# Twelve split weight slots of a two-block transformer kernel, moved from one byte residue modulo 512 to twelve

## The reference

```python
def _swiglu(t, w_gate, w_up, w_down):
    return (jax.nn.silu(t @ w_gate) * (t @ w_up)) @ w_down

def first_block(x, mem, ...):
    for l in range(DEPTH):                                  # DEPTH = 2
        h = h + 0.5 * _rmsnorm(_swiglu(...ffn1...), ...)    # 1024 -> 2816 -> 1024
        proj = u @ w_in[l]                                  # three kinds of attention
        ...
        merged = g_sb * (o_sb @ w_br_sb) + g_fx * (o_fx @ w_br_fox) + g_mem * (o_mem @ w_br_mem)
        h = h + _rmsnorm(merged @ w_out[l], ...)
        h = h + 0.5 * _rmsnorm(_swiglu(...ffn2...), ...)

def second_block(x, ...):
    # layer 0: short convolution mixer; layer 1: latent attention; each with a
    # convolutional FFN: (silu(g) * u) @ w_down, where g, u = conv(x_n @ w_up)
    ...
    return rms_norm(h, final_norm)
```

## Time and profile before

| | |
|---|---|
| median of 3 runs | 1845.45 us (1845.1 to 1845.69) |
| span of the profiled execution | 1842.3 us |
| TensorE matmul | 1829.0 us busy, 99%, 10951 instructions |
| TensorE weight load | 1633.5 us busy, 89% |
| VectorE | 1287.1 us, 70% |
| ScalarE | 1090.7 us, 59% |
| GpSimd | 205.1 us, 11% |
| DMA | 333.94 MB, mean 181 GB/s |

### The profile page before, as it was taken

How to read it: one execution, slowest core, us unless ns; L and a number is a source line. 1 busy time by engine, 2 the same in 40 slices (tenths; PEclk the granted TensorE clock), 3 DMA queues, 4 the chain that set the end, 5 groups by cost and what they waited for, 6 DMA issues and landing times.

```text
span 1842.3 us, 28823 instructions
## 1 busy us (share of the span) xinstructions
PE 1829.0 (99%) x10951; PEld 1633.5 (89%) x10951; DVE 1287.1 (70%) x2041; ACT 1090.7 (59%) x1885; POOL 205.1 (11%) x158
## 2 busy tenths in 40 slices
PE   8999999999999999999999999999999999999998
PEld 7888999998888888888999888888889998989997
DVE  6775747787777568755777788755768765768763
ACT  7665545555666466645555657655557654757653
POOL 0220001110022002200011102210002210001210
PEclk9999999999999999999999999999999999999999
DMA  9755565455576558664654548654747654537663
GB/s 268 216 186 183 172 194 171 140 158 176 173 225 192 189 148 233 186 193 139 196 176 143 186 146 230 193 190 144 226 139 215 187 195 155 173 115 205 198 192 103
DMA packets 435721, 333.94 MB, mean 181 GB/s; under 512 B 25338, under 2 KB 381312, under 8 KB 435584
## 3 DMA queue, kind: packets, MB, share of 16 engines
q1 hardware_dynamic: 435008, 331.57, 59.7%
q10 hardware_dynamic: 576, 0.53, 0.1%
HBM read 330.97 MB, written 1.05 MB: 180 GB/s over the span
## 4 chain that ended last, share of the span: by engine, by line
PE 96%; DVE 2%; ACT 1%; issue 0%; DMA 0%; ACTq 0%
PE bank L1759 16%; PE bank L1736 15%; PE bank L1738 15%; PE bank L1737 15%; PE bank L1747 7%; PE bank L1761 7%; PE bank L1748 7%; PE bank L1749 7%; PE bank L1765 2%; PE bank L1758 1%; DVE wlo L1106 1%; PE bank L2017 0%; DVE U L1159 0%; PE bank L2083 0%; PE bank L2088 0%; PE bank L2054 0%
## 5 line engine op out<-in xcount | busy, mean ns | idle before, releaser
L1106 DVE TENSOR_TENSOR wlo<-raw,whi 128x1024 fp32r<-128x1024 f32 (+3 forms) x637 | 760.9, 1202 | 286.3 <-ACT whi L578 276.8
L578 ACT ACTIVATE whi<-raw 128x1024 fp32r<-128x1024 f32 (+3 forms) x637 | 645.6, 1023 | 324.6 <-PE bank L1738 247.9
L1759 PE MATMUL bank<-U,whi 128*128 128x512 f32 x1280 | 439.2, 395 | 0.2 <-DVE wlo L1106 0.2
L1761 PE MATMUL bank<-U,wlo 128*128 128x256 f32 x1120 | 314.6, 281 | 0.0
L1747 PE MATMUL bank<-U,whi 128*128 128x256 f32 x1024 | 289.2, 282 | 0.0
L1748 PE MATMUL bank<-U,whi 128*128 128x256 f32 x1024 | 286.1, 279 | 0.0
L1749 PE MATMUL bank<-U,wlo 128*128 128x256 f32 x1024 | 286.0, 279 | 0.0
L1759 PEld LDWEIGHTS bank<-U,whi 128*128 128x128 f32 x1280 | 230.2, 188 | 42.9 <-DVE wlo L1106 0.7
L1736 PE MATMUL bank<-whi,U 128*128 128x384 f32 (+2 forms) x592 | 219.2, 370 | 2.7 <-DVE wlo L1464 2.1
L1736 PE MATMUL bank<-whi,hhi 128*128 128x512 f32 x560 | 219.3, 392 | 0.0
L1738 PE MATMUL bank<-wlo,hhi 128*128 128x512 f32 x560 | 218.1, 390 | 0.0
(11 more groups left out here) (309 smaller groups left out, 2367.4 us busy)
## 6 DMA issues: line engine op xcount, KB each, us to landing
raw<-in_ffn_w_up SPq DMA_DIRECT2D x351, 256.0 KB, 3.5
raw<-in_ffn_w_down SPq DMA_DIRECT2D x264, 256.0 KB, 2.9
raw<-in_ffn_w_gate SPq DMA_DIRECT2D x175, 256.0 KB, 3.4
raw<-in_w_gate SPq DMA_DIRECT2D x128, 192.0 KB, 2.9
raw<-in_w_in SPq DMA_DIRECT2D x80, 256.0 KB, 3.4
raw<-in_a_w_in SPq DMA_DIRECT2D x48, 256.0 KB, 3.2
raw<-in_w_mem_kv SPq DMA_DIRECT2D x32, 256.0 KB, 3.3
raw<-in_w_out SPq DMA_DIRECT2D x32, 256.0 KB, 3.1
```

The lines of the kernel that those rows point to most:

```text
L578: act.activation(whi[n % SLOTS][:, 0:w], raw[n % RAW][:, 0:w], ACT.Copy).then_inc(hi_ready, 1)
L1106: dve.tensor_tensor(wlo[n % SLOTS][:, 0:w], raw[n % RAW][:, 0:w], whi[n % SLOTS][:, 0:w].bitcast(F32), ALU.subtract).then_inc(lo_ready, 1)
L1759: ins = pe.matmul(dst, wh, u2[:, k, :], start=(k == 0), stop=(k == KT - 1))
L1761: pe.matmul(dst[:, 0:TOK], wl, uhi[:, k, :], start=False, stop=False)
```

## The change

Behind each of the twelve split slots stands a filler of 8 float32 (32 bytes), and high and low slots alternate: whi0, wlo0, whi1, wlo1, and so on. A last filler of 128 bytes makes 512 bytes in all, so that everything behind the slots moves by 512 bytes and keeps its residue. raw stays where it was.

```diff
+SLOT_GAP = 8
...
         raw = [sb(f"raw{s}", [P, CW]) for s in range(RAW)]
-        whi = [sb(f"whi{s}", [P, CW], F32R) for s in range(SLOTS)]
-        wlo = [sb(f"wlo{s}", [P, CW], F32R) for s in range(SLOTS)]
+        whi, wlo = [], []
+        for s in range(SLOTS):
+            for name, slots in (("whi", whi), ("wlo", wlo)):
+                slots.append(sb(f"{name}{s}", [P, CW], F32R))
+                sb(f"{name}_gap{s}", [P, SLOT_GAP])
+        sb("slot_rest", [P, P - 2 * SLOTS * SLOT_GAP])
```

## The result

| | before | after |
|---|---|---|
| median | 1845.49 us (1845.1 to 1845.69, 4 runs) | 1854.74 us (1853.66 to 1855.09, 4 runs) |
| span of the profiled execution | 1842.3 us | 1852.7 us |

The changed kernel is slower: ratio 1.0052, 95% interval 1.004 to 1.0064, +9.25 us. The forecast was 1854.8 us.

A forecast was written before the change was run, and what follows sets the result against it. TensorE, 99% busy at full clock, was taken to bound the kernel, so time is a sum of pitches. Terms 11.6 - 2.0 + 1.1 - 1.4 = +9.3 us on 1845.45 gave 1854.8 us, range 1834 to 1866.

The forecast's parts named there:

- What bounds the kernel: TensorE, 99% busy at 2.4 GHz and hardly waiting; time is a sum of 10951 matmul pitches; splits delay it under 1 us.
- That only the residues act, not the order: Whole kernel: no instruction, wait or DMA added or removed, costing nothing; the change acts only through addresses' effect on pitches.
- Kind 1: 2424 matmuls, down product included, weights moving and activation standing at 128: +11.6 us, bounds 0 and 14.2.
- a price by distance: For TensorE's operand residues, shorter way round 512: 0 free, 32 to 128 half, 160 or more all of 6.6 ns.
- Kind 2: Matmuls of 512, 384 and 344 columns, weights moving and U standing at 448: -2.0 us.
- Kinds 3 and 4: Projections, weights standing and 256 columns moving: +1.1 us; 160 wide chunks mixing 512 and 256 columns: -1.4 us.
- Faster: The 113.3 ns rhythm spreads through projections and wide chunks, gaining more than 512-column matmuls lose: 1833 us; chance 0.28.
- No change: The 6.6 ns may belong to U itself at 448, so weights' addresses change little: 1845 us; chance 0.16.
- Slower, twice as far: Every unequal 512-column matmul pays 6.6 ns, 256 columns go to 120.0: +24 us, 1870 us; within the 0.56 case.

The follow-up runs named there:

- added rounds: Kernel before with groups of 24 matmuls, real rounds among them, added behind its last one; down round 227, 231.7, 226 and 233.3 ns by low and high offsets.
- the list: Kernel before plus 768 matmuls behind its last, 24 per fixed operand pair, standing address stepped by 32 bytes; 512 columns: 226.7 ns at 0, 233.3 at 32.

## Why the prediction was right, and where its steps were not

**What bounds the kernel:** right. TensorE's share, clock and waits are those of before, and the split costs what it did (1226 ns); the loss is in the pitches. Two readings beside it were off. The splits hold TensorE up for 2.6 us in all, not for under 1: L1464 is the split of the first chunk. And the 3.15 us between span and median are not all the ends of the span: in every run whose own time is on record that gap is 1.8 us, so the profiled execution of before was also some 1.3 us faster than the median.

**That only the residues act, not the order:** right, as the run with the slots alternating at one residue shows.

**Kind 1, the term that carries the sum:** its size is right, +10.6 for +11.6 us, and that is luck. The step below it, a price by distance (0 nothing, 32 to 128 half, 160 and more all), holds only in that 0 is cheap. 32 bytes cost all of it (all slots at 160: 233.3 ns), 256 nothing (at 384: 226.7), and the standing operand 192 ahead 2.2 of 6.6. The share I charged was 0.72 on average; the trace has (231.8 - 226.7) / 6.6 = 0.77 in the down product. It came out near because slots 4 and 5 were charged too much (all of the price, for 0.64 and 0.76 by the pitches below) and slots 0 and 1 too little (0.17 and 0.5, for 0.71 and 0.79).

The sign that this step was wrong was in the changed kernel's own profile. I had said that slot 0 should stay near 226.7 and slots 3 to 5 be at 233. The starts of four chunks of the down product, of slots 0, 1, 3 and 4 (a chunk is twelve matmuls; to the next chunk it is 2.77 us from slot 0, 2.80 from slot 3, 2.77 from slot 4):

```profile
643.34 0.39 PE L1741 MATMUL bank<-whi,hhi 128*128 128x512 f32 x1
...
646.11 0.39 PE L1741 MATMUL bank<-whi,hhi 128*128 128x512 f32 x1
...
651.67 0.40 PE L1741 MATMUL bank<-whi,hhi 128*128 128x512 f32 x1
...
654.47 0.39 PE L1741 MATMUL bank<-whi,hhi 128*128 128x512 f32 x1
```

By slot, in this down product, the pitches are 231.4, 231.9, 230.9, 233.7, 230.9 and 231.7 ns. Slot 0 pays 4.7 of the 6.6 ns, although two thirds of its matmuls are at difference 0. The added rounds give 231.7 for slot 0 and 233.3 for slot 3. So what I missed is that a matmul's pitch depends on the ones before it. Slot 2 shows that this is not yet a rule to calculate with: its differences, 128 and 96, cost 6.6 and 7.6 in the list, and it reads 230.9. No added group had its round; why it is cheaper stays open.

**Kind 2:** the right sign, -0.8 for -2.0 us. U standing at 448 was already at difference 64, a full price; whi5 at 448 and whi1 at 192, 256 bytes away, are at difference 0, but their low parts and the slots around them are not. With 384 and 344 columns nothing was gained (-0.1), for the -1.0 I took.

**Kinds 3 and 4:** +1.0 for +1.1, and -1.3 for -1.4. Here too the numbers are luck. Of the +1.9 for projections with U at 448, the 1920 in the convolutional FFNs were to bring +1.3 and brought +0.4; those of the attention were to bring +0.6 and brought +1.5. Five of their chunks ran at 113.3 ns before, and none does after. Slot 5 was to read 120 and reads 118.3. As for the wide chunks, U at 128, equal residues everywhere, made them slower, where my step said faster.

**The rivals.** "Faster" did not happen, but its mechanism is real: with U at 320 the rhythm of 113.3 ns fills the projections and the kernel is faster than before. The twelve residues did the opposite: they took it away where it was. "No change", an operand's own place as the cause, fell: absolute places don't matter, to 0.1 ns. "Slower, twice as far" shows with all slots at 320 (1864 us), where the down product pays 6.6 ns a matmul; the changed kernel has slots at difference 0 and 192 and rounds near 231, and stays below.

## What to carry to other kernels

When TensorE is full, read its pitch from start times, not its busy share, and compare stretches that run the same code on different tiles. The start addresses of the standing and the moving operand modulo 256 were worth 3% of a pitch at 512 columns (226.7 or 233.3 ns) and up to 6% at 256 (113.3 or 120.0). Here they were best equal in a loop of 512-column matmuls alone; loops with short ones, the mixed wide chunk above all, have to be tried out, each with its real round, because one matmul with another difference slows those behind it. Spreading the buffers over many residues took away the one good difference: 231.8 ns, near the dear end.

## What the runs showed of the hardware

TensorE's pitch with float32r operands in SBUF, for one pair of addresses repeated, depends on (standing minus moving start address) modulo 256, tried in steps of 32 bytes, and not on the place: eight absolute residues and eight offsets by multiples of 512 bytes agree to 0.1 ns. Settled pitches are 226.7 or 233.3 ns at 512 columns and 113.3 or 120.0 at 256, or a mean of a repeating pattern around them. In cycles of 2.4 GHz that is 544 and 560 for 512 columns, 272 and 288 for 256: 16, 32 or 48 cycles above the number of columns. The Trainium skill ("SBUF — State Buffer", section "Who interferes with whom") says that TensorE never waits on another engine for SBUF; nothing here contradicts that, since the added down round ran alone at the 226.7 ns that it has in the kernel beside VectorE, ScalarE and the DMAs. Its "TensorE: Matmul & The Clock Gate", section "Step-by-step: what each phase is for", has the next weight load take nothing from a running matmul; here the pitch of weight load and matmul changes with the relative address of the two, 226.7 or 233.3 ns, which two wholly independent reads would not explain. Which read is held up by which, no run shows.

The difference alone does not settle the pitch. Behind a change of difference it took up to ten matmuls to settle again (above). With the same difference of 64 and 256 columns, a repeated pair of fixed addresses ran at 117.8 ns and the projection round at 113.3, to the end of their groups. In the kernel before, of 94 whole projection chunks with U at 448, five ran at 113.3 (the stretch of the earlier trace rows runs into one of them) and 89 at 117.7 to 117.9; with all slots at 384, the same differences, it was six, in partly other places. And with all slots at 320 the first convolutional FFN had 120.0 ns and the second 118.7. What decides between two rhythms was not tested by itself. Two windows of the run with the added rounds, projections with U at 320 and at 448, 18 pitches each:

```profile
2098.92:2100.96 2.04, 2.04 (x20) 1.00 0.00 0
2110.20:2112.32 2.12, 2.12 (x20) 1.00 0.00 0
```

That the two reads of TensorE collide in parts of SBUF that repeat every 256 bytes would fit the period. The runs show the period and the prices; the mechanism behind them is only argued.
